# A ring of 21 row buffers, and the last tile's value rows added by VectorE alone in PSUM

## What is computed

```
for each head (8): top 16 of 16384 experts by product keys -> idx (b, h, k), softmax gate g
ue = u[idx]                                   # rows of 1024, gathered per token
ve = v[idx]
act = gelu(einsum('bd,bhkd->bhk', x, ue))
out = einsum('bhk,bhkd->bd', g * act, ve)     # sum of 8 * 16 = 128 value rows per token
```

## Time and profile before

| | |
|---|---|
| median of 3 runs | 3704.34 us (3693.79 to 3711.89) |
| profiled execution, its own time | 3682.36 us |
| its span in the trace | 3680.6 us |
| busy: PE / VectorE / ScalarE / POOL | 91% / 80% / 41% / 57% |
| mean granted TensorE clock | 0.959 of full speed |
| rows of tiles 4 to 7 in the trace | about 2906 us to 3675 us |

### The profile page before, as it was taken

The page is one execution under the profiler, slowest core; times in us unless marked ns, Lnnn a source line. Parts: engine busy times, 40 slices in busy tenths (PEclk is TensorE's granted clock), DMA queues, the critical chain, the costliest instruction groups (busy, mean ns, idle before and its releaser), DMA issues. The chain is left out here.

```text
span 3680.6 us, 46234 instructions
## 1 busy us (share of the span) xinstructions
PE 3349.9 (91%) x13366; PEld 2201.6 (60%) x13366; DVE 2935.0 (80%) x6932; ACT 1507.0 (41%) x3205; POOL 2102.3 (57%) x1831
## 2 busy tenths in 40 slices
PE   8999899999999978998799999999968799999977
PEld 7787555544444446766688887888844355555522
DVE  4499664377987977999988898888889798986754
ACT  5225585122442322333454454454434344444422
POOL 6221134055565656777766676666666666566665
PEclk9999999999999989999899999999988899999998
DMA  6415564698999998999999999999999999999998
GB/s 214 127 40 147 138 181 163 206 367 315 358 377 376 345 390 335 369 384 373 406 401 401 378 407 406 393 402 395 392 401 370 362 373 401 384 400 385 349 372 328
DMA packets 443320, 1224.46 MB, mean 333 GB/s; under 512 B 65250, under 2 KB 153478, under 8 KB 442047
## 3 DMA queue, kind: packets, MB, share of 16 engines
q0 software_dynamic: 239616, 872.52, 61.7%
q1 hardware_dynamic: 177162, 313.45, 24.6%
q10 hardware_dynamic: 26293, 35.54, 2.8%
HBM read 1129.03 MB, written 92.31 MB: 332 GB/s over the span
## 5 line engine op out<-in xcount | busy, mean ns | idle before, releaser
L2682 POOL DMA_INDIRECT late_v_rows<-in_peer_v,late_kept_idx x573 | 545.1, 951 | 239.6 <-issue 157.4
L2669 POOL DMA_INDIRECT late_u_rows<-in_peer_u,late_kept_idx x320 | 490.7, 1534 | 266.5 <-DVE late_dots L3275 194.8
L3275 DVE CUSTOM_DVE_ANT_0 late_u_rows<-late_u_rows,open_rows_ps 128x1024 f32<-128x1024 f32 x432 | 522.0, 1209 | 9.3 <-DMA late_u_rows<-in_peer_u,late_expert_idx 8.9
L3310 DVE SCALAR_TENSOR_TENSOR late_x<-late_v_rows,late_weights,late_x 128x1024 f32<-128x1024 f32 x368 | 471.0, 1280 | 0.0
L2824 PE MATMUL open_q_and_scores_ps<-table_h_T_upper,table_u_T_upper 128*128 128x512 f32 x1024 | 424.7, 415 | 0.0
L2824 PE MATMUL open_q_and_scores_ps<-table_h_T_lower,table_u_T_upper 128*128 128x512 f32 x1024 | 403.1, 394 | 0.0
L2824 PE MATMUL open_q_and_scores_ps<-table_h_T_upper,table_u_T_lower 128*128 128x512 f32 x1024 | 401.7, 392 | 0.0
L2682 POOL DMA_INDIRECT late_u_rows<-in_peer_v,late_kept_idx x259 | 244.9, 946 | 145.3 <-issue 57.1
L1844 POOL DMA_INDIRECT open_u_rows<-in_peer_u,late_expert_idx x115 | 164.5, 1430 | 254.9 <-DVE late_dots L2284 127.9
L3020 ACT ACTIVATE table_u_T_upper<-open_h_T_ps 128x512 fp32r<-128x512 f32 x256 | 152.4, 595 | 232.7 <-PE open_h_T_ps L2802 199.8
L2907 PE MATMUL open_sums_ps<-late_v_rows,table_diag 128*128 128x512 f32 (+1 forms) x382 | 206.1, 664 | 43.8 <-ACT table_diag L3086 18.4
(11 more groups left out here) (475 smaller groups left out, 7970.7 us busy)
## 6 DMA issues: line engine op xcount, KB each, us to landing
table_u_block<-in_peer_u SPq DMA_DIRECT2D x128, 512.0 KB
scr_scores<-table_scores SPq DMA_DIRECT2D x32, 1024.0 KB
open_weight_columns<-in_w_in SPq DMA_DIRECT2D x64, 256.0 KB
table_first_scores<-scr_scores SPq DMA_DIRECT2D x4, 4096.0 KB
table_second_scores<-scr_scores SPq DMA_DIRECT2D x4, 4096.0 KB
front_w_raw<-in_w_in SPq DMA_DIRECT2D x48, 256.0 KB, 5.8
scr_m<-open_gated SPq DMA_DIRECT2D x42, 256.0 KB
late_v_rows<-in_peer_v,late_kept_idx POOLq DMA_INDIRECT x573
```

The lines of the kernel that those rows point to most:

```text
L2669: pool.indirect_dma_start(u[k % U_RING][:], None, io["peer_u"][0], bass.IndirectOffsetOnAxis(ap=rows_of(n), axis=0)).then_inc(s_u[k % U_RI ...
L2682: pool.indirect_dma_start(slot[:], None, io["peer_v"][0], bass.IndirectOffsetOnAxis(ap=rows_of(m), axis=0)).then_inc(arrived, 16)
L3275: dve.tensor_tensor_reduce(u[k % U_RING][:], u[k % U_RING][:], h2_rows, 1.0, 0.0, ALU.mult, ALU.add, dots[:, n % COLS:n % COLS + 1]).then_ ...
L3310: dve.scalar_tensor_tensor(rows[:], slot[:], weight_of(m), rows[:], ALU.mult, ALU.add).then_inc(s_vsum, 1)
```

## The change

Two things. First, the ring of value rows of tabled tiles grows from 14 buffers to 21. The seven new ones (`more`) are buffers whose earlier use is over by then: two halves of the transposed keys, `merged_T`, `h_T`, the norm gain, `h` and the row buffer `h2_next`. POOL waits once, at the first of them, for all their earlier readers. From then on row m waits for row m - 21 instead of m - 14. Their arrival semaphores are ones that the stage before has done with (`rings_spent`).

Second, in the last tile `by_columns` is no longer true. `by_vector` is true for each of its 128 steps, `by_tensor` for none: VectorE adds all 1024 columns of each row to both banks of `open_sums_ps` with one instruction; TensorE's 128 row matmuls and ScalarE's 128 diagonals of the tile are gone. Tiles 4 to 6 are shared by columns as before.

```diff
+LANE_SLOTS = 7
+ALL_SLOTS = U_RING + V_RING + LANE_SLOTS
...
 def by_columns(m):
-    return m >= GATHER_END
+    return GATHER_END <= m < STEPS - TILE_STEPS
 def by_vector(m):
-    return m < SHORT_START or m % 2 == 0 or by_columns(m)
+    return m < SHORT_START or m >= GATHER_END or m % 2 == 0
 def by_tensor(m):
-    return m >= SHORT_START and (m % 2 == 1 or by_columns(m))
+    return by_columns(m) or SHORT_START <= m < GATHER_END and m % 2 == 1
...
+    s_more = [Spent(*done.rings_spent[k]) for k in range(LANE_SLOTS)]
+    more = [keysT[:, NH * k:NH * (k + 1), :].rearrange("p k n -> p (k n)") for k in range(2)]
+    more += [mT[:].rearrange("p k t -> p (k t)"), h2T[:].rearrange("p k t -> p (k t)"), gain[:], h2[:], h2_next[:]]
...
         def v_row(m):
-            before = m - (V_RING if m < GATHER_END else U_RING + V_RING)
-            if GATHER_END <= m < GATHER_END + U_RING:
-                pool.wait_ge(s_dot, S0 + DOTS[GATHER_END] - U_RING + m - GATHER_END + 1)
+            j = m - GATHER_END
+            before = m - (V_RING if j < 0 else U_RING + V_RING if j < U_RING + V_RING else ALL_SLOTS)
+            if 0 <= j < U_RING:
+                pool.wait_ge(s_dot, S0 + DOTS[GATHER_END] - U_RING + j + 1)
+            elif U_RING + V_RING <= j < ALL_SLOTS:
+                if j == U_RING + V_RING:
+                    pool.wait_ge(s_sc, S0 + HEADS)
...
             elif before >= AHEAD_ROWS:
                 if by_vector(before):
                     pool.wait_ge(s_vsum, S0 + VECTOR_SUMS[before] + 1)
                 if by_tensor(before):
                     pool.wait_ge(s_sum, S0 + TENSOR_SUMS[before] + 1)
...
             if t in TABLED:
-                half = banks_of(t)[:, 0, :]
+                wide = BANK if by_columns(m) else D
+                sums = banks_of(t)[:].rearrange("p a n -> p (a n)")[:, 0:wide]
                 if m == tile_start(t):
-                    dve.tensor_scalar(half, slot[:, 0:BANK], weight_of(m), None, ALU.mult).then_inc(s_vsum, 1)
+                    dve.tensor_scalar(sums, slot[:, 0:wide], weight_of(m), None, ALU.mult).then_inc(s_vsum, 1)
                 else:
-                    dve.scalar_tensor_tensor(half, slot[:, 0:BANK], weight_of(m), half, ALU.mult, ALU.add).then_inc(s_vsum, 1)
+                    dve.scalar_tensor_tensor(sums, slot[:, 0:wide], weight_of(m), sums, ALU.mult, ALU.add).then_inc(s_vsum, 1)
```

More of the change, by code:

```diff
@@ L2412, in opening @@
     done.s_iota = s_iota
+    done.rings_spent = [(s, 16 * sum(b == k for b, _, _ in U_PLACES)) for k, s in enumerate(s_u)]
+    done.rings_spent += [(s, 16 * sum(b == k for b, _, _ in V_PLACES)) for k, s in enumerate(s_v)]
     done.spent = [(s, S0 + 16 * 8) for b in range(2) for s in s_chunk[b]] + [(s, S0 + 16) for s in (s_xT0, s_yin, s_gain, s_x)]
@@ L2512, in v_slot @@
         if j < 0:
-            return s_v[k % V_RING], v[k % V_RING], k // V_RING + 1
-        turn, i = j // (U_RING + V_RING), j % (U_RING + V_RING)
+            return s_v[k % V_RING], v[k % V_RING][:], k // V_RING + 1
+        turn, i = j // ALL_SLOTS, j % ALL_SLOTS
         if i < U_RING:
             d = DOTS[GATHER_END] + i
-            return s_u[d % U_RING], u[d % U_RING], d // U_RING + 1 + turn
+            return s_u[d % U_RING], u[d % U_RING][:], d // U_RING + 1 + turn
+        if i >= U_RING + V_RING:
+            return s_more[i - U_RING - V_RING].sem, more[i - U_RING - V_RING], turn + 1 + s_more[i - U_RING - V_RING].start // 16
         d = GATHER_END - AHEAD_ROWS + i - U_RING
-        return s_v[d % V_RING], v[d % V_RING], d // V_RING + 1 + turn
+        return s_v[d % V_RING], v[d % V_RING][:], d // V_RING + 1 + turn
     def row_in(eng, m):
@@ L3307, in vector_sum @@
                 dve.wait_ge(s_h2, S0 + NE + 1)
-                dve.tensor_scalar(rows[:], slot[:], weight_of(m), None, ALU.mult).then_inc(s_vsum, 1)
+                dve.tensor_scalar(rows[:], slot, weight_of(m), None, ALU.mult).then_inc(s_vsum, 1)
             else:
-                dve.scalar_tensor_tensor(rows[:], slot[:], weight_of(m), rows[:], ALU.mult, ALU.add).then_inc(s_vsum, 1)
+                dve.scalar_tensor_tensor(rows[:], slot, weight_of(m), rows[:], ALU.mult, ALU.add).then_inc(s_vsum, 1)
         def weights(G):
```

8 lines of the change are left out of this document (7 added, 1 removed).

## The result

The changed kernel takes 3708.43 us, median of 20 runs (3698.20 to 3725.59); the kernel before takes 3697.45 us, median of 20 (3687.57 to 3711.89). The ratio is 1.0030, 95% interval 1.0018 to 1.0041: slower by 11 us (6.7 to 15.2). The forecast was 7 us less than before, so the change went the other way, though the time itself lies inside the stated range of 3674 to 3720. The profiled execution of the changed kernel took 3713.14 us (span 3711.1, mean granted clock 0.932). That of before, 3682.36 us, lies 15 us under its own median of 20, so the two profiles must not be subtracted from each other: they are 31 us apart where the medians are 11 apart.

The account below looks back on a forecast made before the run. It took VectorE and TensorE to bound tiles 4 and 5, TensorE tile 6, and the supply of rows tile 7. +1.8 - 8.8 = -7.0 us on 3704.34 gave 3697 us, range 3674 to 3720.

Parts of the forecast that it names:

- the ring's term of -8.8 us: Ends of tiles 4 and 5: rows lying ready would be added at 0.89 us each, saving 4.9 and 3.9 us.
- TensorE is full: Tile 6: TensorE sets the pace, busy 177 of 189 us, and neither adding engine waits for a row.
- The wide rows' term of +1.8 us: Tile 7: VectorE alone becomes the bound, 1.285 us a row, period 1.425 us, ending 1.8 us later than before.
- VectorE waits for no row: Sign expected in tile 7's trace: no waits of VectorE for arriving rows, where before they were 55.7 us.
- The rival of the dear row: Tile 7: PSUM's two banks charged apart, 1.64 us a row, 27.5 us more, kernel at 3725 us; chance 0.12.
- The gap of 0.14 us: Tile 7: hand-over between successive rows on VectorE, added to the 1.285 us instruction for a period of 1.425 us.
- GpSimd, said to wait for VectorE after each row: Sign expected in tile 7's trace: POOL waits for VectorE after each row instead of issuing every 1.24 us.
- The premise under that term: Tile 7 before: 182 us instead of 164, the missing 18 us being interruptions that begin on ScalarE.
- The starting time: Whole kernel before the change: median 3704.34 us, from which the forecast subtracted 7.0 us.
- Tile 7's first row was to start 9 us earlier: Sign expected in the trace: time gained at the ends of tiles 4 and 5 moves tile 7's start 9 us earlier.

Follow-up runs that it names:

- quiet kind: Sets of runs in which the kernel before takes 3646 and 3645 us, with no wait of ScalarE put down to "remote" from 2900 us on.
- set 3: Ring of 21 alone, VectorE alone in tile 7 with 14 buffers, and two alternating sums there with 14 or 21, on one chip; kernel before 3699.88 us.
- disturbed kind: Sets of runs in which the kernel before takes 3691 to 3700 us and ScalarE's waits put down to "remote" sum to 62 to 186 us.
- e9: Kernel before with only the ring grown to 21, tile 7 still shared by columns: 3706.04 us, ratio 1.0015.
- e14: Changed kernel, with GpSimd also limited to six gathers under way: 3729.75 us, ratio 1.0110 to the kernel before.
- e13: Kernel before (ring of 14), with GpSimd limited to six gathers under way: 3717.73 us, ratio 1.0078.
- e17: Changed kernel (ring of 21) with two alternating sums for tile 7's wide rows and earlier diagonals in tiles 4 to 6: 3645.45 us, ratio 0.9999 to before.
- e18: Changed kernel but ring of 14, with two alternating sums in tile 7 and earlier diagonals in tiles 4 to 6: 3646.03 us, ratio 1.0005 to before.

## Why the prediction was wrong

**The step that failed is the ring's term of -8.8 us.** The prediction said: "I take it whole, since behind each place VectorE or TensorE sets the pace and passes the time on", with bounds from -8.8 to 0. Measured alone, the ring is +5.5 us (1.5 to 10.0) in the kind in which both kernels were compared, outside these bounds, and -4.7 us in the quiet kind, about half of the size. The rows did lie ready, at 0.89 us a row. But the time was not passed on: VectorE's idle time moved from the rows to the picks, and grew. Behind the rows stood neither VectorE's nor TensorE's own work but a chain of hand-overs, TensorE's spread, ScalarE's hot rows and diagonals, TensorE's pick and rows, VectorE's mask. Busy shares of 90% had hidden it. "TensorE is full", said of tile 6, was a misreading: it was busy 177 us of 189, and in the quiet kind the same tile takes 173.6 us with TensorE busy throughout. VectorE's waits in the trace of before, tiles 4 to 6, would have shown the chain:

```profile
DVE table_masked L3351 <- DMA scr_mqT<-front_turned: 56.4, 22, 6.1
DVE open_rows_ps L3304 <- DMA late_v_rows<-in_peer_v,late_kept_idx: 2.4, 2, 1.6
DVE open_sums_ps L3304 <- DMA late_v_rows<-in_peer_v,late_kept_idx: 2.3, 3, 1.3
```

Whatever the names, VectorE stands idle 62 us ahead of masks there and 13 ahead of rows. The size put on the term, two ends of tiles added up, was one of places, and what lay between them had another bound.

**The wide rows' term of +1.8 us held in this kind.** Duration 1.288 against 1.285, period 1.42 against 1.425, tile 7 182.8 us against 183 to 184; measured alone +2.6 us (-2.2 to 7.0). VectorE waits for no row, as said. The rival of the dear row is out. The Trainium skill ("VectorE: DVE Perf Modes", the section on the TRN2 errata) would have the row 65 ns dearer out of PSUM than in SBUF; 1.288 against 1.280 us is 8 ns, so for this form the measurement decides against it. The gap of 0.14 us from one dependent row's end to the next one's start was right for the sum; that dependence costs 0.23 us against rows that may overlap is a thing the prediction didn't ask. GpSimd, said to wait for VectorE after each row, has only 11 waits put down to VectorE's rows, 5.5 us; the rest of its idle time is called "issue", a name that a missing record can give.

**The premise under that term held for one kind only.** The 18 us by which tile 7 exceeded 128 x 1.28 were called interruptions that begin on ScalarE. The quiet sets fit that: where no late start of ScalarE is seen, a shared tile 7 takes 162.4 us (with 21 buffers). They also show that the same term is +19 us there. The prediction took 182 us of one execution as the tile's time and asked only what would replace the interruptions, not whether they are always there.

**The starting time.** 3704.34, the median of three runs, was 7 us above the median of 20. The forecast 3697 therefore equals the time before, by accident. That 3708 lies within 3674 to 3720 says little for the working too: around the true 3697 the range had room for 23 us either way.

**Not seen:** a rival in which the ring costs time. Tile 7's first row was to start 9 us earlier. In set 3 it starts 9.5 us later with the ring of 21 than with 14 (3517.0 and 3507.6), of which 2.0 us were there before tile 4 began.

**Open:** why 21 buffers lengthen tile 6 by 8 us in the disturbed kind. It isn't the wide rows (e9 has none), and with at most six gathers under way the tile is still longer, 202.0 against 197.1 us (e14, e13, one profile each). The time is seen in TensorE's idle time ahead of rows. Why TensorE waits longer there with more buffers, by the lead in landed rows or by the places of the new buffers in SBUF, no run separates; 21 against 14 buffers with earlier diagonals would tell whether the cost goes where these waits go, but that pair (e17, e18) ran in a quiet set.

## What to carry to other kernels

Buffers pay only where the thing that arrives late is what they hold. Before a deeper ring is given a gain, sum the waits of the consuming engine by what it waits for; if another wait (here for the picks, over four times that for rows) stands behind the first, the gain can turn into it. A wait chain over three engines is sensitive to anything that delays one hand-over, and taking an engine out of the chain can be worth more than the work it did: shared rows took 162 to 164 us or 180 to 186 by circumstance, rows on one engine with two sums 160 to 167. One profiled execution is one draw: profile the unchanged kernel again beside each experiment, before a difference is explained. And where a profile names who ended a wait, see first whether its records are complete (do the gathers have a time to landing?), or go by idle times.
